# Adding each expert tile's rows to X in DRAM, instead of storing the tile and gathering two rows per token afterwards

## The chip, the cores and the metric

The kernel runs on one core of one Trainium2 chip. The metric is the device time of one execution in microseconds. The kernel before took 1797.72 us (median of 3 runs, 1793.24 to 1802.61).

## The reference, cut to what matters

Two layers over 1024 tokens of 1024 float32 features. Each layer has a mixer and then a mixture of 16 experts, of which every token takes 2; its two weighted results are added to x.

```python
def grouped_moe(h, router_w, router_bias, w_gate, w_up, w_down):
    ...
    _, idx = lax.top_k(masked, TOP_K)                    # 2 experts of one group
    ...
    a = jax.nn.silu(einsum(t, w_gate)) * einsum(t, w_up)
    y = jnp.einsum('tef,efd->td', a * gates[:, :, None], w_down)

for l in range(DEPTH):
    ...                                                  # mixer: x = x + g1 * y
    h = modulate(rms_norm(x, norm_ffn_g[l]), sh2, sc2)
    x = x + g2[:, None, :] * grouped_moe(h, ...)
return rms_norm(x, final_norm_g)
```

## The kernel before, in words

X stays in SBUF as 8 blocks of 128 tokens by 1024 features. The kernel is five programs, one for each engine (PE, VectorE = DVE, ScalarE = ACT, GpSimd = POOL, SyncE = SP), written by hand in program order; semaphores order them against each other. No scheduler moves anything.

**The expert stage of a layer.** DVE sorts the 2048 pairs of token and expert into tiles of 128 slots, one expert a tile (route, L1268). Here that gives 25 tiles in layer 0 and 26 in layer 1. A slot that no pair fills has token 0 and weight 0. The normed rows lie in DRAM (xn_scratch). For each tile POOL gathers its 128 rows of 4 KB into XG by an indirect DMA (L581). PE then runs this loop (L1050): gate and up products of tile t (L1015), transposes of tile t+1 (L996), down product of tile t-1 (L1030), transposes of tile t's hidden values (L1022). DVE multiplies the down product by the slot's weight and the layer's gate row into YS (L1435, L1437), one buffer of 512 KB. ACT stores YS into y_scratch, a DRAM tensor with a row per slot (L691). Before DVE writes YS again it waits for that store (L1433, y_out). SP loads the experts' weights, 3 MB each, into three buffers; it issues a load when the last tile of the expert in that buffer has its down product (L450).

**The stretch after the tiles.** POOL waits for the last store and issues 16 indirect gathers (L607): for each block of X the rows of its tokens' first and second slot. DVE adds both to the block (L1174 by combine). ACT sums each block's squares (L651) and takes roots four blocks at a time (L653). After layer 0, DVE scales four blocks (L1240), PE transposes them (L869), ACT and DVE evict the transposed half into HTR (L660, L1251), then the same for the second half; then the product with conf_w1 begins (L886). Its 16 items come in the order of w1_group: the first two need the first half of the tokens only. After layer 1, DVE writes scaled output blocks (L1244), four at a time, and SP stores them (L514).

**Other places that the change touches.** x_pieces on ACT (L698) reads the pieces of X that the mixer's output product finishes. At the start POOL writes zeros into the rows of y_scratch that a short run of tiles would leave unwritten (L561, 7.68 MB).

Of the kernel before, what the change touches and what calls it, by code (L numbers as in the profile page):

```python
# [7 lines left out]
F32 = mybir.dt.float32  # L8
I32 = mybir.dt.int32
U32 = mybir.dt.uint32  # L10
# [5 lines left out]
P = 128  # L16
# [4 lines left out]
NL = 2  # L21
# [108 lines left out]
def trunk(nc, i, out):  # L130
    with ExitStack() as ctx:
# [35 lines left out]
        TCUR = sb("TCUR", [P, 1], U32)  # L167
        RT = sb("RT", [1, 2 * MAXT], I32)
# [73 lines left out]
        def hv(n):  # L242
            return HTR[:, n, :]

        Y1, Y2 = ([HTR[:, 3 * n + b, :] for b in range(3)] + [R[:, 3 - n, b * D:(b + 1) * D] for b in range(4)]
                  for n in range(2))
        NY0, NY = 3, 7

        def y_of(b):

            return b if b < NY else NY0
# [11 lines left out]
        xn_dram = nc.dram_tensor("xn_scratch", (T, D), F32, kind="Internal").ap()  # L263
        y_dram = nc.dram_tensor("y_scratch", (MOST * P, D), F32, kind="Internal").ap()
# [38 lines left out]
        xup = sem("x_updated")  # L303
# [40 lines left out]
        c_in = [[[sem(f"combine_in{l}_{b}_{s}") for s in range(2)] for b in range(NB)] for l in range(NL)]  # L344
# [66 lines left out]
        def _(sp):  # L411
# [54 lines left out]
            sp.wait_ge(zeroed, 16 * (NH + 1))  # L466
            nt = experts(0)
            sp.wait_ge(dn[0], nt)
# [23 lines left out]
            for n in range(2):  # L492
                weights1(n)
# [6 lines left out]
            sp.wait_ge(c_in[0][NB - 1][1], 16)  # L500
# [10 lines left out]
            experts(1)  # L511
# [7 lines left out]
        def _(pool):  # L519
# [35 lines left out]
            rest = y_dram[LEAST * P:MOST * P, :].rearrange("(t p) d -> p t d", p=P)  # L555
            zeros = ZERO.unsqueeze(1).broadcast_to([P, MOST - LEAST, HT])

            for q in range(16):
                if q == 4:
                    for h in range(NH):  # L560
                        pool.dma_start(rest[:, :, HT * h:HT * h + HT], zeros).then_inc(zeroed, 16)  # L561
                    pool.dma_start(glu_dram.rearrange("(c p) t -> p c t", p=P)[:, :, 0:PADC],
                                   ZERO[:, 0:KC * PADC].rearrange("p (c t) -> p c t", c=KC)).then_inc(zeroed, 16)
# [6 lines left out]
            for l in range(NL):  # L570
# [7 lines left out]
                nt = pool.value_load(RT[0:1, 0:1], min_val=1, max_val=MOST)  # L578
# [5 lines left out]
                pool.tensor_tensor(PSCR[:, l:l + 1], PSCR[:, 2:3], PSCR[:, 2:3], ALU.add).then_inc(held[l], 1)  # L584
                pool.tensor_copy(TCUR[:], TOKI[:, 0:1]).then_inc(cur_ok[l], 1)
                pool.wait_ge(cur_ok[l], 1)
                gather()
                with pool.Fori(0, nt) as t:
# [4 lines left out]
                    pool.wait_ge(held[l], t + 1)  # L593

                    pool.tensor_tensor(PSCR[:, l:l + 1], PSCR[:, 2:3], PSCR[:, 2:3], ALU.add).then_inc(held[l], 1)
                    gather()

                pool.wait_ge(zeroed, 16 * (NH + 1))
                pool.wait_ge(y_out[l], nt * 16 + 16)
                pool.wait_ge(xg_in[l], nt * 16 + 16)  # L600
                pool.wait_ge(held[l], nt + 1)
                pool.tensor_tensor(PSCR[:, l:l + 1], PSCR[:, 2:3], PSCR[:, 2:3], ALU.add).then_inc(held[l], 1)
                for b in range(NB):
                    if b == NY:
                        pool.wait_ge(xup, 8 * l + NY0 + 1)
                    for s, dst in ((0, Y1), (1, Y2)):
                        pool.indirect_dma_start(  # L607
                            out=dst[y_of(b)], out_offset=None, in_=y_dram,
                            in_offset=bass.IndirectOffsetOnAxis(ap=SLOTU[:, s, b:b + 1], axis=0)
                        ).then_inc(c_in[l][b][s], 16)  # L610
# [14 lines left out]
        def _(act):  # L625
# [18 lines left out]
            def rms_sums(r, h):  # L644
# [3 lines left out]
                for b in range(4 * h, 4 * h + 4):  # L648
                    if r:
                        act.wait_ge(xup, 8 * (r // 2 - 1) + b + 1)  # L650
# [17 lines left out]
            def experts(l):  # L668
# [13 lines left out]
                act.sem_inc(y_out[l], 16)  # L682
# [6 lines left out]
                def store(t):  # L689
                    act.wait_ge(ys_d[l], t + 2)  # L690
                    act.dma_start(y_dram[bass.ds(t * P, P), :], YS).then_inc(y_out[l], 16)  # L691
                hidden(0)
                with act.Fori(1, nt) as t:
                    hidden(t)
                    store(t - 1)
                store(nt - 1)

            def x_pieces(l, g0):  # L698

                for p in range(4):  # L700
# [6 lines left out]
                    act.wait_ge(xpj, 16 * l + 4 * p + 4)  # L707
                    for b in (2 * p, 2 * p + 1):
# [47 lines left out]
            for h in range(NH):  # L756
                rms_sums(2, h)
            for h in range(NH):
                evict_ht(2, 1, 0, h)
            for n in range(16):  # L760
# [4 lines left out]
                act.activation(SIG[n % 2], take(g)[:], ACT.Sigmoid,  # L765
                               bias=PT[:, COL_B1 + KC + ct:COL_B1 + KC + ct + 1]).then_inc(free["A"], 1)
            act.wait_ge(conv_ok, KC)
# [24 lines left out]
            rms_sums(4, 0)  # L792
            rms_sums(4, 1)
# [3 lines left out]
        def _(pe):  # L797
# [307 lines left out]
            transposes(2, 1)  # L1105
# [31 lines left out]
            for n in range(16):  # L1137
                c, h = w1_group(n)
                ht_ready(2, h)
# [24 lines left out]
        def _(dve):  # L1164
# [68 lines left out]
            def rms_apply(r, h):  # L1233
# [4 lines left out]
                for b in range(4 * h, 4 * h + 4):  # L1238
                    if r < 4:
                        dve.tensor_scalar(XN[h][:, b % 4, :], X[:, b, :], RSTD[:, b:b + 1], None,  # L1240
                                          ALU.mult).then_inc(xn_ok, 1)
                        continue
# [431 lines left out]
```

## Time and profile before

| | us |
|---|---|
| median of 3 runs | 1797.72 |
| the profiled execution, its own time | 1794.08 |
| span in the profile, first to last instruction | 1792.3 |
| PE busy | 1525.7 (85%) |
| DVE busy | 855.2 (48%) |
| ACT busy | 257.8 (14%) |
| POOL busy | 146.8 (8%) |
| moved by DMA | 300.79 MB, mean 168 GB/s |

An engine's busy time is the sum of its instructions' durations, weight loads of PE apart. The granted clock is TensorE's, as a share of full speed. The start of a row is counted from the first instruction.

### The profile page before, as it was taken

Reading aid. Unit: us, or ns where it says so; the run is one execution under the profiler, and the core shown is the slowest. Engines: PE = TensorE matmul, PEld = TensorE weight load, DVE = VectorE, ACT = ScalarE, POOL = GpSimd, SP = SyncE. Lnnn points to the kernel's source line nnn. Section 1 sums busy time; section 2 is a strip of 40 time slices with the busy share of each in tenths; the row PEclk is TensorE's granted clock in tenths of the full one; section 3 lists DMA queues with packets and bytes.
Section 4 is the critical chain, followed back from the end, with each engine's and each line's share of the span. In section 5 each row is a group of like instructions: output and inputs, shape, how many; then the busy total and the mean of one; then the engine's idle time right before and its main releaser. Section 6 shows DMA issues by size and latency. Waiting matters only on the chain.

```text
span 1792.3 us, 16755 instructions
## 1 busy us (share of the span) xinstructions
PE 1525.7 (85%) x5355; PEld 851.1 (47%) x5356; DVE 855.2 (48%) x1546; ACT 257.8 (14%) x507; POOL 146.8 (8%) x267
## 2 busy tenths in 40 slices
PE   3899999989965999999459989987999389999980
PEld 2684544448853444444134434432887244444440
DVE  3554686644234223222352999975333523332226
ACT  2210000001121111111130000003212111111112
POOL 2000000000000111011210000000000101111104
PEclk9999999999986999999769989998999599999995
DMA  9575067460044666875532336433002658466827
GB/s 337 163 273 164 24 202 232 156 220 1 16 177 160 216 237 229 283 270 192 192 138 65 100 75 149 106 90 101 1 1 98 254 195 302 164 226 237 286 97 284
DMA packets 196430, 300.79 MB, mean 168 GB/s; under 512 B 12021, under 2 KB 153425, under 8 KB 196384
## 3 DMA queue, kind: packets, MB, share of 16 engines
q1 hardware_dynamic: 169952, 205.94, 36.6%
q0 software_dynamic: 17696, 62.24, 9.7%
q10 hardware_dynamic: 8736, 31.99, 4.5%
q8 instruction: 30, 0.49, 0.1%
q14 instruction: 16, 0.13, 0.0%
HBM read 248.51 MB, written 51.53 MB: 167 GB/s over the span
## 4 chain that ended last, share of the span: by engine, by line
PE 73%; DVE 13%; DMA 7%; ACT 2%; issue 2%; POOL 1%; SPq 0%; DVEq 0%; POOLq 0%; ACTq 0%
PE bank L886 19%; PE bank L1015 18%; PE bank L964 15%; PE bank L1030 9%; DVE W L1196 3%; DVE R L1620 3%; DMA W<-in_moe_w_down 3%; PE bank L996 3%; DVE R L1174 2%; PE bank L1122 1%; DMA W<-in_ada_w 1%; PE bank L869 1%; PE bank L1041 1%; PE bank L1155 1%; PE bank L903 1%
## 5 line engine op out<-in xcount | busy, mean ns | idle before, releaser
L886 PE MATMUL bank<-HTR,W 128*128 128x512 f32 x1024 | 449.8, 597 | 7.4 <-DVE R L1607 7.4
L1015 PE MATMUL bank<-W,R 128*128 x784 | 349.9, 600 | 17.8 <-DMA W<-in_moe_w_down 13.8
L886 PEld LDWEIGHTS bank<-HTR,W 128*128 128x128 f32 x1024 | 193.4, 191 | 243.8 <-issue 243.1
L1174 DVE TENSOR_TENSOR R<-bank,R 128x256 f32<-128x256 f32 (+1 forms) x91 | 49.3, 541 | 523.9 <-ACT R L686 322.3
L964 PE MATMUL bank<-W,R 128*128 128x256 f32 x1024 | 231.1, 385 | 9.0 <-ACT R L786 7.8
L1015 PEld LDWEIGHTS bank<-W,R 128*128 128x128 f32 x784 | 147.0, 193 | 186.2 <-issue 186.2
L964 PEld LDWEIGHTS bank<-W,R 128*128 128x128 f32 x1024 | 194.7, 193 | 38.6 <-ACT R L786 8.7
L1620 DVE SCALAR_TENSOR_TENSOR R<-R,PT 128x998 f32<-128x998 f32 (+21 forms) x152 | 195.0, 1283 | 5.4
L1030 PE MATMUL bank<-W,R 128*128 x408 | 185.4, 598 | 3.9 <-DVE R L1428 3.9
L1196 DVE SCALAR_TENSOR_TENSOR W<-W,CAB 128x256 f32<-128x256 f32 x308 | 149.3, 485 | 11.0
L1030 PEld LDWEIGHTS bank<-W,R 128*128 128x128 f32 x408 | 74.1, 192 | 78.4 <-issue 78.4
L1435 DVE SCALAR_TENSOR_TENSOR R<-bank,GSLOT,HTR 128x512 f32<-128x512 f32 x51 | 38.3, 751 | 121.8 <-PE bank L1030 121.8
L678 ACT ACTIVATE R<-bank,MC 128x128 f32<-128x128 f32 x212 | 79.7, 456 | 95.9 <-PE bank L996 95.9
L686 ACT ACTIVATE R<-bank 128x256 f32<-128x256 f32 x51 | 19.6, 384 | 477.6 <-PE bank L1015 459.9
L1411 DVE TENSOR_SCALAR R<-bank,MC 128x128 f32<-128x128 f32 x212 | 72.4, 403 | 18.6 <-PE bank L996 18.6
L869 PE MATMUL bank<-IDENT,R 128*128 128x128 f32 x128 | 28.0, 386 | 62.2 <-DVE R L1240 45.7
L1174 DVE TENSOR_TENSOR R<-R 128x512 f32<-128x512 f32 (+8 forms) x146 | 64.5, 461 | 24.6 <-ACT R L751 21.3
L996 PEld LDWEIGHTS bank<-IDENT,R 128*128 128x128 f32 x424 | 51.0, 144 | 42.9 <-issue 26.9
L996 PE MATMUL bank<-IDENT,R 128*128 128x128 f32 x424 | 56.8, 278 | 15.6 <-DMA R<-xn_scratch,TCUR 15.6
L964 PE MATMUL bank<-W,HTR 128*128 128x256 f32 x256 | 59.9, 394 | 2.4 <-ACT HTR L660 1.4
L869 PEld LDWEIGHTS bank<-IDENT,R 128*128 128x128 f32 x128 | 21.1, 197 | 71.1 <-issue 35.0
L964 PEld LDWEIGHTS bank<-W,HTR 128*128 128x128 f32 x256 | 50.0, 198 | 10.1 <-issue 1.9
(194 smaller groups left out, 972.5 us busy)
## 6 DMA issues: line engine op xcount, KB each, us to landing
W<-in_ada_w SPq DMA_DIRECT2D x48, 1024.0 KB, 11.5
W<-in_moe_w_gate SPq DMA_DIRECT2D x32, 1024.0 KB, 7.6
W<-in_moe_w_up SPq DMA_DIRECT2D x32, 1024.0 KB, 11.3
W<-in_moe_w_down SPq DMA_DIRECT2D x32, 1024.0 KB, 13.5
y_scratch<-R ACTq DMA_DIRECT2D x51, 512.0 KB, 7.4
W<-glu_scratch SPq DMA_DIRECT2D x48, 258.0 KB, 4.7
W<-in_conf_w SPq DMA_DIRECT2D x12, 1024.0 KB, 8.8
W<-in_hyb_w_in SPq DMA_DIRECT2D x10, 1024.0 KB, 13.1
```

The lines of the kernel that those rows point to most:

```text
L678: ins = act.activation(XT[:, k, :], TB_[0][:, k * P:(k + 1) * P], ACT.Identity, bias=MC[:, l, 3, k:k + 1], scale=MC[:, l, 2, k:k + 1])
L869: ins = pe.transpose(TB_[q % 2][:, P * b:P * b + P], XN[h][:, b, P * k:P * k + P], IDENT[:])
L886: ins = pe.matmul(dst[:], lhs(k), rhs(k), start=(k == 0), stop=(k == kc - 1))
L964: ins = pe.matmul(dst[:, QW * b:QW * b + QW], src[:, k, t0:t0 + P], w[:, k, :], start=(k == 0), stop=(k == KC - 1))
L996: ins = pe.transpose(TB_[k // 4][:, P * (k % 4):P * (k % 4) + P], XG[:, P * k:P * k + P], IDENT[:])
L1015: ins = pe.matmul(M[0][:], XT[:, k, :], W[:, bass.ds(at + k * 2 * FE, 2 * FE)], start=(k == 0), stop=(k == KC - 1))
L1030: ins = pe.matmul(M[1 + h][:], AT[:, k, :], W[:, bass.ds(at + 2 * KC * FE + k * D + h * HT, HT)], start=(k == 0), stop=(k == 1))
L1174: return dve.tensor_tensor(o, a, b, op)
L1196: ins = dve.scalar_tensor_tensor(out=acc, in0=w[:, k, :], scalar=CAB[:, k, 0:1], in1=acc, op0=ALU.mult, op1=ALU.add)
L1411: ins = dve.tensor_scalar(XT[:, k, :], TB_[1][:, (k - 4) * P:(k - 3) * P], MC[:, l, 2, k:k + 1], MC[:, l, 3, k:k + 1], ALU.mult, ALU.add)
L1435: dve.scalar_tensor_tensor(out=YS[:, 0:HT], in0=M[1][:], scalar=g, in1=GBF[:, 0:HT], op0=ALU.mult, op1=ALU.mult)
L1620: link(dve.scalar_tensor_tensor(out=o[:, d:T], in0=p[:, 0:T - d], scalar=tap(CTAPS - 1 - d), in1=o[:, d:T], op0=ALU.mult, op1=ALU.add))
```

## The change

DRAM now holds a copy of X (xsum_scratch), which ACT writes from SBUF while the mixer finishes X. After each expert tile POOL adds the 128 rows of YS to the rows of that copy by one indirect DMA that accumulates. It does so after it has issued the gather of the tile three further on. YS is still one buffer, and DVE waits before it for the previous add. Two adds never overlap, since POOL waits for the one before. Empty slots now point at 128 spare rows behind the 1024 real ones, a row of its own for each partition, in both scratch tensors, so that no row occurs twice in a tile. The loop runs over the tiles but two (more = tiles - 2), and two adds follow it. After the last add SP loads X's 8 blocks back. y_scratch, its zeros, the ACT stores, the 16 gathers and the 16 additions of DVE are gone. In layer 0 the second half's transposes and evictions move behind the first two items of the conf_w1 product. At the end roots, scaling and output go block by block.

```diff
@@ POOL, expert tiles
-                with pool.Fori(0, nt) as t:
+                def next_tile(t):
                     pool.wait_ge(xg_in[l], t * 16 + 16)
                     pool.tensor_copy(TCUR[:], TOKI[:, bass.ds(t + 1, 1)]).then_inc(cur_ok[l], 1)
                     pool.wait_ge(cur_ok[l], t + 2)
                     pool.wait_ge(xtr[l], t + 1)
...
-                pool.wait_ge(y_out[l], nt * 16 + 16)
-                for b in range(NB):
-                    for s, dst in ((0, Y1), (1, Y2)):
-                        pool.indirect_dma_start(
-                            out=dst[y_of(b)], out_offset=None, in_=y_dram,
...
+                def add_rows(t):
+                    pool.wait_ge(y_out[l], t * 16 + 16)
+                    pool.tensor_copy(TSUM[:], TOKI[:, bass.ds(t, 1)]).then_inc(sum_cur[l], 1)
+                    pool.wait_ge(sum_cur[l], t + 1)
+                    pool.wait_ge(ys_d[l], t + 2)
+                    met()
+                    pool.indirect_dma_start(
+                        out=xs_dram, out_offset=bass.IndirectOffsetOnAxis(ap=TSUM[:, 0:1], axis=0),
+                        in_=YS, in_offset=None, compute_op=ALU.add).then_inc(y_out[l], 16)
...
+                next_tile(0)
+                next_tile(1)
+                pool.wait_ge(x_out[l], 16 * 4)
+                with pool.Fori(0, more) as t:
+                    next_tile(t + 2)
+                    add_rows(t)
+                add_rows(more)
+                add_rows(more + 1)
@@ ACT, per tile
-                def store(t):
-                    act.wait_ge(ys_d[l], t + 2)
-                    act.dma_start(y_dram[bass.ds(t * P, P), :], YS).then_inc(y_out[l], 16)
@@ ACT, x_pieces
+                    act.dma_start(xs_dram[2 * P * p:2 * P * (p + 1), :].rearrange("(b q) d -> q b d", q=P),
+                                  X[:, 2 * p:2 * p + 2, :]).then_inc(x_out[l], 16)
@@ SP
+            def reload(l, nt, b):
+                if b == 0:
+                    sp.wait_ge(y_out[l], nt * 16 + 16)
+                sp.dma_start(X[:, b, :], xs_dram[P * b:P * b + P, :]).then_inc(x_back[b], 16)
             nt = experts(0)
-            sp.wait_ge(dn[0], nt)
-            for n in range(2):
-                weights1(n)
+            for b in range(NB):
+                reload(0, nt, b)
+                if b == 3:
+                    for n in range(2):
+                        weights1(n)
@@ PE, after layer 0
             transposes(2, 0)
-            transposes(2, 1)
             for n in range(16):
+                if n == 2:
+                    transposes(2, 1)
@@ DVE, route: spare rows for empty slots
+                tokr = SM[:, 0:16].rearrange("p (s b) -> p s b", s=TOPK)
+                link(dve.tensor_scalar(SPARE[:], TOKF[:, 0:1], float(T), None, ALU.add))
+                for s in range(TOPK):
+                    dve.scalar_tensor_tensor(out=tokr[:, s, :], in0=TOKF[:], scalar=-float(T),
+                                             in1=rf.rearrange("p (s b) -> p s b", s=TOPK)[:, s, :],
+                                             op0=ALU.add, op1=ALU.subtract).then_inc(dch, 1)
@@ DVE, the end
+            def last_norm(b):
+                dve.wait_ge(fin_sd, b + 1)
+                link(dve.reciprocal(RSTD[:, b:b + 1], SD[:, b:b + 1]))
+                dve.scalar_tensor_tensor(out=OUTS[b], in0=X[:, b, :], scalar=RSTD[:, b:b + 1],
+                                         in1=FGB, op0=ALU.mult, op1=ALU.mult).then_inc(out_ok, 1)
```

The order of POOL's instructions in layer 0, from the loop over the tiles to the end of the stage. Before, TCUR and PSCR are the small copies around a gather, and y_scratch is read in two runs behind the loop:

```order
L590 COPY TCUR<-TOKI 128x1
L591 REGISTER_ALU
L595 TENSOR_TENSOR PSCR<-PSCR 1x1
L581 DMA R<-xn_scratch,TCUR 128x1024
L588 REGISTER_ALU
L588 COMPARE_AND_BRANCH
L599 ISA
L601 REGISTER_ALU
L602 TENSOR_TENSOR PSCR<-PSCR 1x1
L607 DMA HTR<-y_scratch,SLOTU 128x1024 x6
L607 DMA R<-y_scratch,SLOTU 128x1024 x10
```

After the change, in the same place, the loop and the first of the two adds behind it:

```order
L598 COPY TCUR<-TOKI 128x1
L599 REGISTER_ALU
L593 TENSOR_TENSOR PSCR<-PSCR 1x1
L588 DMA R<-xn_scratch,TCUR 128x1024
L606 ISA
L607 ISA
L607 COPY TSUM<-TOKI 128x1
L608 REGISTER_ALU
L593 TENSOR_TENSOR PSCR<-PSCR 1x1
L611 DMA xsum_scratch<-R,TSUM 1152x1024
L622 REGISTER_ALU
L622 COMPARE_AND_BRANCH
```

Each turn of the loop now issues a gather and, behind it on the same queue, an add; the 16 gathers behind the loop have become two adds.

The order of PE's instructions between the experts of layer 0 and the conf_w1 product, before (the transposes are the rows with IDENT, the product those with HTR, and L1122 is the first convolution by PE):

```order
L1030 MATMUL bank<-W,R 128x512
L1056 REGISTER_ALU
L869 MATMUL bank<-IDENT,R 128x128 x64
L886 MATMUL bank<-HTR,W 128x512 x64
L1122 MATMUL bank<-W 32x512 x16
```

And after the change:

```order
L1050 MATMUL bank<-W,R 128x512
L1076 REGISTER_ALU
L889 MATMUL bank<-IDENT,R 128x128 x32
L906 MATMUL bank<-HTR,W 128x512 x32
L889 MATMUL bank<-IDENT,R 128x128 x32
L906 MATMUL bank<-HTR,W 128x512 x32
L1142 MATMUL bank<-W 32x512 x16
```

Half of the 64 transposes now stand behind the first 32 matmuls of the product.

## Rows read from the trace of the kernel before

**Rows 1.** The page, busy time of PE: us, share of the span, instructions.
```profile
PE 1525.7 (85%) x5355; PEld 851.1 (47%) x5356; DVE 855.2 (48%) x1546; ACT 257.8 (14%) x507; POOL 146.8 (8%) x267
```
**Rows 2.** Chain of waits: start us, us, what; the last store of either layer.
```profile
873.45 7.08 DMA y_scratch<-R
...
1745.73 2.67 DMA y_scratch<-R
```
**Rows 3.** Timeline after layer 0's tiles: start us, us, engine, line, operation [idle before].
```profile
866.66 0.74 DVE L1437 SCALAR_TENSOR_TENSOR R<-bank,GSLOT,HTR 128x512 f32<-128x512 f32 x1
...
871.87 0.75 DVE L1435 SCALAR_TENSOR_TENSOR R<-bank,GSLOT,HTR 128x512 f32<-128x512 f32 x1 [4.14 <-PE bank L1030]
...
881.37 0.96 POOL L607 DMA_INDIRECT HTR<-y_scratch,SLOTU  x1 [0.51 <-issue]
...
898.27 1.06 ACT L651 ACTIVATE R<-X 128x1024 bf16<-128x1024 f32 x1 [1.52 <-DVE X L1174]
...
899.44 1.28 ACT L653 ACT_TABLE_LOAD   x1
...
901.35 4.03 DVE L1240 TENSOR_SCALAR R<-X,RSTD 128x1024 f32<-128x1024 f32 x4
...
924.60 6.76 PE L869 MATMUL bank<-IDENT,R 128*128 128x128 f32 x28 [3.77 <-DVE R L1240]
...
932.09 13.47 PE L886 MATMUL bank<-HTR,W 128*128 128x512 f32 x31
```
**Rows 4.** Windows: stretch, its length, busy us of each engine, granted clock, DMA share, GB/s.
```profile
740.00:800.00 60.00, 51.91 (x144) 24.64 (x144) 15.72 (x35) 7.54 (x20) 5.55 (x13) 0.94 0.84 287
...
872.00:905.00 33.00, 0.00 (x0) 0.00 (x0) 17.21 (x17) 7.33 (x12) 19.05 (x19) 0.57 0.94 312
```
**Rows 5.** Timeline of the end, after layer 1's tiles.
```profile
1737.24 0.74 DVE L1437 SCALAR_TENSOR_TENSOR R<-bank,GSLOT,HTR 128x512 f32<-128x512 f32 x1
...
1744.15 0.75 DVE L1435 SCALAR_TENSOR_TENSOR R<-bank,GSLOT,HTR 128x512 f32<-128x512 f32 x1 [5.83 <-PE bank L1030]
...
1771.53 17.79 SPq L514 DMA_DIRECT2D out<-R  x8
...
1784.09 4.87 DVE L1244 SCALAR_TENSOR_TENSOR R<-X,RSTD,HTR 128x1024 f32<-128x1024 f32 x4
```
**Rows 6.** DMA by line: issues, size, median us from issue to landing.
```profile
W<-in_moe_w_down SPq DMA_DIRECT2D x32, 1024.0 KB, 13.5
y_scratch<-R ACTq DMA_DIRECT2D x51, 512.0 KB, 7.4
...
HTR<-gate_scratch ACTq DMA_DIRECT2D x2, 512.0 KB, 3.8
```
**Rows 7.** The gathers of tiles (tile TCUR): time to landing of all 53.
```profile
DMA to landing us min/median/max: 4.0/4.6/7.8
```
**Rows 8.** Timeline of one expert tile in layer 0.
```profile
831.80 0.75 DVE L1435 SCALAR_TENSOR_TENSOR R<-bank,GSLOT,HTR 128x512 f32<-128x512 f32 x1 [2.28 <-PE bank L1030]
...
836.83 0.18 POOL L590 COPY TCUR<-TOKI 128x1 uint32 x1 [6.96 <-DMA R<-xn_scratch,TCUR]
...
838.47 1.04 PE L996 MATMUL bank<-IDENT,R 128*128 128x128 f32 x8
...
839.16 0.42 DVE L1174 TENSOR_TENSOR R<-bank,R 128x256 f32<-128x256 f32 x1 [5.62 <-ACT R L686]
...
843.20 0.75 DVE L1435 SCALAR_TENSOR_TENSOR R<-bank,GSLOT,HTR 128x512 f32<-128x512 f32 x1 [2.28 <-PE bank L1030]
```
**Rows 9.** Waits: PE in the gate and up products, us in total, times, longest.
```profile
PE bank L1015 <- DMA W<-in_moe_w_down: 13.8, 4, 4.4
```
**Rows 10.** Chain of waits: the first gate and up product of layer 0.
```profile
566.77 9.97 PE bank L1041 x16
```
**Rows 11.** Timeline of DVE at the start of layer 0's route.
```profile
524.37 0.18 DVE L1499 RECIPROCAL RSTD<-SD 128x4 f32<-128x4 f32 x1 [1.43 <-ACT SD L712]
```

More of the change, by code:

```diff
@@ L243, in hv @@
             return HTR[:, n, :]
[L245 to L251, printed above, removed]
         GBF = hv(6)
@@ L343, in trunk @@
         y_out = [sem(f"tile_stored{l}") for l in range(NL)]
-        c_in = [[[sem(f"combine_in{l}_{b}_{s}") for s in range(2)] for b in range(NB)] for l in range(NL)]
+        x_out = [sem(f"x_rows_stored{l}") for l in range(NL)]
+        x_back = [sem(f"x_block_reloaded{b}") for b in range(NB)]
+        sum_cur = [sem(f"sum_tokens_copied{l}") for l in range(NL)]
+        fin_sd = sem("final_root_ready")
         out_ok = sem("output_block_ready")
@@ L466, in _ @@
             sp.wait_ge(zeroed, 16 * (NH + 1))
+            for l in range(NL):
+                sp.wait_ge(y_out[l], 16)
+            def reload(l, nt, b):
+                if b == 0:
+                    sp.wait_ge(y_out[l], nt * 16 + 16)
+                sp.dma_start(X[:, b, :], xs_dram[P * b:P * b + P, :]).then_inc(x_back[b], 16)
             nt = experts(0)
-            sp.wait_ge(dn[0], nt)
             def weights1(n):
@@ L510, in _ @@
             sp.wait_ge(free["D"], emptied(GROUPS["var"] - 1))
-            experts(1)
+            nt = experts(1)
+            for b in range(NB):
+                reload(1, nt, b)
             for b in range(NB):
@@ L560, in _ @@
                     for h in range(NH):
-                        pool.dma_start(rest[:, :, HT * h:HT * h + HT], zeros).then_inc(zeroed, 16)
+                        s = slice(HT * h, HT * h + HT)
+                        pool.dma_start(xn_dram[T:T + P, s], ZERO).then_inc(zeroed, 16)
+                        pool.dma_start(xs_dram[T:T + P, s], ZERO).then_inc(y_out[h], 16)
                     pool.dma_start(glu_dram.rearrange("(c p) t -> p c t", p=P)[:, :, 0:PADC],
@@ L577, in _ @@
                 pool.wait_ge(xn_out[l], 16 * NB)
-                nt = pool.value_load(RT[0:1, 0:1], min_val=1, max_val=MOST)
+                more = pool.value_load(RT[0:1, 1 + NE:2 + NE], min_val=0, max_val=MOST - 2)
                 def gather():
@@ L583, in gather, with met @@
                         in_offset=bass.IndirectOffsetOnAxis(ap=TCUR[:, 0:1], axis=0)).then_inc(xg_in[l], 16)
[L584 to L587, printed above, removed]
-                with pool.Fori(0, nt) as t:
+                def met():
+                    pool.tensor_tensor(PSCR[:, l:l + 1], PSCR[:, 2:3], PSCR[:, 2:3], ALU.add).then_inc(held[l], 1)
+                def next_tile(t):
                     pool.wait_ge(xg_in[l], t * 16 + 16)
@@ L754, in _, with gate1 @@
             experts(0)
[L756 to L760, printed above, removed]
+            def gate1(n):
                 g = GROUPS["w1"] + 2 * n
@@ L766, in _ @@
                                bias=PT[:, COL_B1 + KC + ct:COL_B1 + KC + ct + 1]).then_inc(free["A"], 1)
+            rms_sums(2, 0)
+            evict_ht(2, 1, 0, 0)
+            rms_sums(2, 1)
+            for n in range(16):
+                if n == 2:
+                    evict_ht(2, 1, 0, 1)
+                gate1(n)
             act.wait_ge(conv_ok, KC)
@@ L791, in _ @@
             experts(1)
-            rms_sums(4, 0)
-            rms_sums(4, 1)
+            for b in range(NB):
+                act.wait_ge(x_back[b], 32)
+                link(act.activation(JUNK, X[:, b, :], ACT.Square, accum_out=SS[:, b:b + 1]))
+                act.activation(SD[:, b:b + 1], SS[:, b:b + 1], ACT.Sqrt, bias=EPSC[:],
+                               scale=1.0 / D).then_inc(fin_sd, 1)
         @block.tensor
@@ L1402, in route @@
                 link(dve.tensor_copy(GSLOT[:], X0[:, MAXT:2 * MAXT]))
-                dve.tensor_copy(TOKI[:], X0[:, 0:MAXT]).then_inc(tab_ok, 1)
+                dve.tensor_scalar(TOKI[:], X0[:, 0:MAXT], SPARE[:], None, ALU.add).then_inc(tab_ok, 1)
             def experts(l):
@@ L1594, in _ @@
             experts(0)
-            for b in range(NB):
-                if b == 5:
-                    rms_apply(2, 0)
-                combine(0, b)
+            rms_apply(2, 0)
             evict_ht(2, 1, 0, 0)
             rms_apply(2, 1)
-            evict_ht(2, 1, 0, 1)
             for n in range(16):
```

62 lines of the change are left out of this document (22 added, 40 removed).

## The prediction

> **What bounds the kernel now.** I read the page's busy times first: PE is busy for 85% of the span [rows 1]. So the change can only pay where PE stands still. The chain of waits then says where. It runs through PE except in a few places, and two of these are the last stores into y_scratch and what follows them [rows 2]. In the first place PE does nothing at all from 872 to 905, while DMA is at its limit: 312 GB/s and a busy share of 0.94, with a mean granted clock of 0.57 [rows 4]. The timeline shows that the conf_w1 product starts only at 932.09 [rows 3]. The end of the kernel has the same shape and nothing after it: 46.7 us from the last YS (1745.6) to the end of the span at 1792.3 [rows 5]. In the tiles a period is 11.4 us, bounded by PE: DVE writes YS at 831.80 and again at 843.20 [rows 8]. DMA is slower than PE there in four places only, where PE waits 13.8 us in all for the weights [rows 9].
>
> **The unknown: one add.** No row shows an accumulating DMA. Let L be its time from POOL's start of it to landing. On an idle chip a gather of the same 512 KB takes 4.0 us at least [rows 7], and a store of 512 KB 2.67 us [rows 2]. An add has to read the old rows and write the new ones. So one row gives the lower bound, 4.0, and for the idle case I take the usual gather and the store one behind the other: about 4.4 + 2.7 = 7.1 us. The upper bound is the slowest gather and the usual store beside weight loads, 7.8 + 7.4 = 15.2 us [rows 6, 7].
>
> The Trainium skill, "DMA: Bandwidth & Descriptors", section "Anatomy of one DMA", fits about 2.0 us plus bytes over 436 GB/s for a DMA issued by GpSimd and puts most of the 2 us on the write receipt. An estimate by it, with the rows read and written once each, is 2.0 + 2.4 us plus about 1 us on POOL, 5.4 us in all. No run here shows it, and by it both terms for the gaps below would be larger by about 3.4 us each.
>
> **The gap after layer 0.** The last YS but one ends at 866.66 + 0.74 = 867.40 [rows 3]. POOL then needs 0.1 to wake, 0.18 for its small instruction and 0.51 from there to the start of the DMA [rows 3, 8], so the add starts at 868.2 and lands at 875.3. DVE has one YS, so its last L1435 starts at 875.4 where it started at 871.87, 3.5 later. YS is done after 1.4 us, the last add starts at 877.5 and lands at 884.6. SP issues the reload at 884.8. The first block lands after 3.8 us, as the loads of 512 KB from DRAM do [rows 6], and the next every 1.7 us (0.524 MB at 312 GB/s [rows 4]): the fourth at 893.7. The four sums follow the blocks, and the last takes 1.25 us; then come the table load of 1.28, the root of 0.3, a reciprocal of 0.2, and four scalings in 4.0 [rows 3]: 900.7. Transposes and evictions of a half took 924.60 to 932.09, 7.5 us. The product begins at 908.2 instead of 932.09: 23.9 us earlier. Its two weight slices are queued behind block 3 and land by 893.7 + 6.7 = 900.4, in time.
>
> Two things are given back. The second half, 7.5 us, now stands in the middle of the product. It is no later than that: its blocks land by 907.1 and its scaling ends near 918, while PE comes to it at 908.2 + 27.6. And the product now starts sooner after PE's idle time, in which the granted clock has a mean of 0.57, near the lower of its levels (1.2 of 2.4 GHz) [rows 4]. The first gate and up product of layer 0, after a similar wait, took 9.97 us [rows 10] where 16 such matmuls at the full clock take 6.95 (13.47 for 31 [rows 3]), so 3.0. Sum: 23.9 - 7.5 - 3.0 = **13.4 us gained**.
>
> **The end.** The same steps from 1737.98 [rows 5]: the add lands at 1745.9, L1435 starts at 1746.0 instead of 1744.15, the last add lands at 1755.3, and the reload is issued at 1755.4. By the engines alone the eighth block would land at 1771.0, take 1.25 + 0.3 + 0.2 + 1.2 us in ACT and DVE, and its store 3.3 (the last one of before, 1789.0 to 1792.3): 1777.3. But 4.19 MB come in and 4.19 MB go out on one SP queue, and 8.39 MB at 312 GB/s are 26.9 us. With 2.1 us before the first bytes and 1 at the end that is 1785.4. I take DMA as the bound: **6.9 us gained**; the engines' bound would be 15.
>
> **The tiles.** POOL has room: it waits nearly the whole period. The add of tile t is issued 0.8 us after YS, behind the gather in POOL's order, so it delays no gather's issue. ACT loses its store, which nothing waited for. The wait in front of YS is the one that can bite. The loop add, YS, add needs L + 1.4 + 0.8 in a period of 11.4, so L may be 9.2 on average. Single adds may be later: DVE idles for 5.6 us after each tile [rows 8], which is its slack. Beside weight loads a store takes 7.4 us against 2.67, so I put a loaded add at 11 and an idle one at 7.1. About half the tiles are loaded (13 loads in 25 and 26 tiles), which gives a mean of 9.1, just inside. I cost the loop at 0.
>
> What it does cost is bandwidth. In the four weight waits the loads have 287 GB/s and a DMA share of 0.84 [rows 4, 9], and one tile's output is in each such load. Reading the old rows adds 0.524 MB, 1.8 us, four times: **7.3 us lost**. Elsewhere a load has 22.8 us or more for 13.5 [rows 6]; that spare time hides it.
>
> **The small edits.** Three more DVE instructions on 8 or 16 columns precede the one-hots in the chain that PE and POOL wait for, 0.2 us each, as the reciprocal on 8 columns takes [rows 11], in two layers: 1.2. The last copy of X's pieces puts an ACT DMA issue of about 0.35 in front of the sums for which DVE waits (1.43 us of idle time [rows 11]): 0.7. Both together **1.9 lost**. The 7.68 MB of zeros go, but PE waits for no DMA at that time: 0. The copies of X, 4.19 MB in each layer, lie beside products that leave DMA mostly idle: 0.
>
> **Sum.** -13.4 - 6.9 + 7.3 + 1.9 = -11.1 us from the profiled execution's own 1794.08: 1783. That execution is 3.6 us under the median, so from the median it would be 1786.6. I forecast 1785. Each us of L counts four times, since each gap holds two adds: at L = 4.0 the DVE waits vanish and the sum is 1773, and without the bandwidth term 1766; at an idle L of 9.2 it is 1791.
>
> **The rivals.**
> *The add becomes the loop's bound (slower).* Place: DVE's wait for y_out before L1435, then PE's down product. It decides from a mean L of 9.2. At a mean of 10 it costs 0.8 x 51 tiles = 41 us and 12 more in the gaps: 1836. With both upper bounds (15.2 loaded, 9.2 idle: mean 12.2) it is 3.0 x 51 = 153 and more, over 1900. For it: my mean of 9.1 stands a tenth under the limit, and a loaded store takes nearly three times an idle one. Against it: the fastest stores leave a wide margin.
> *The gather becomes late (slower).* A gather now queues behind an add on POOL's queue. At 836.83 it had landed and at 838.47 PE used it: 1.6 us of slack in a loaded tile [rows 8]. If the add delays it by 3 us, 26 loaded tiles lose 1.4 each, 36 us: 1819.
> *The gaps gain little (no change).* If reloads and stores behind the adds run at less than the gathers' rate, or the clock stays low for longer in the conf_w1 product, some 10 us of the gain go: 1794.
> *A short add (faster still).* L near 5 and an end where both directions overlap: 1783 - 8 - 5 = 1770.
>
> For the second the Trainium skill speaks too: "DMA: Bandwidth & Descriptors", section "Queues, rings and completion order", says that within a queue of one DMA engine descriptors are taken in order, while different queues take turns packet by packet. The stores of before had ACT's queue for themselves, and the adds share POOL's with the gathers. Whether that costs anything no row of before shows, as nothing else was on that queue during the tiles.
>
> **How the numbers follow.** The forecast has 0.40, with its own range of 1776 to 1793; the late add 0.22, the late gather 0.10, little gained 0.17, the short add 0.11. A measurement of this kernel can't tell less than 0.5%, 9 us, from no change: faster means under 1788.7, slower over 1806.7. Of the forecast 0.32 lies under 1788.7 and 0.08 above. Faster: 0.32 + 0.11 + a little of the others = 0.45. Slower: the two slow rivals, and some of what I can't see of an operation that no row shows, 0.35. The same: 0.20. The range goes from the short add to a mean L a little over 10, 1768 to 1845.
>
> **What would show it.** Right: adds that land in about 7 us where no weights load and 11 where they do; no wait of DVE before YS that PE feels; L1435 of the last tiles later by 3.5 and 1.8 us; the conf_w1 product starting some 31 us after the last YS instead of 59; the end taking 38 us from the last YS. Wrong: a tile period over 11.4 us with DVE waiting for the add, PE's transposes waiting for gathers, or weight waits far over 13.8 + 7.3 us. The forecast is wrong above all if L is not what a gather and a store make together.

## The result, and the profile after

The changed kernel takes 1768.44 us (median of 4 runs, 1763.36 to 1769.91) beside 1795.48 for the kernel before on the same chip (4 runs, 1792.55 to 1802.61): ratio 0.985, 95% interval 0.983 to 0.988. Five more runs later, beside other variants, gave 1767.63 and a ratio of 0.983 (0.981 to 0.985). The profiled execution took 1768.09 us with a span of 1766.3, so 26.0 us less in either than before. The sum of the prediction was 11.1 less from that base. The sign was right, the size was less than half of what came.

The page's busy times of the changed kernel, against [rows 1]: PE does the same work, and DVE and POOL exchange some.

```profile
PE 1524.5 (86%) x5355; PEld 848.0 (48%) x5356; DVE 818.0 (46%) x1528; ACT 259.1 (15%) x513; POOL 214.0 (12%) x388
```

The timeline after layer 0's tiles, for [rows 3]: start, duration, engine and line, and in brackets the idle time before and what ended it.

```profile
879.23 0.75 DVE L1460 SCALAR_TENSOR_TENSOR R<-bank,GSLOT,HTR 128x512 f32<-128x512 f32 x1 [6.42 <-DMA xsum_scratch<-R,TSUM]
879.90 0.74 DVE L1462 SCALAR_TENSOR_TENSOR R<-bank,GSLOT,HTR 128x512 f32<-128x512 f32 x1
...
881.06 1.57 POOL L611 DMA_INDIRECT xsum_scratch<-R,TSUM  x1 [0.16 <-issue]
887.26 1.77 SPq L470 DMA_DIRECT2D X<-xsum_scratch  x4
...
890.61 1.06 ACT L668 ACTIVATE R<-X 128x1024 bf16<-128x1024 f32 x1 [21.68 <-DMA X<-xsum_scratch]
...
898.65 2.74 DVE L1261 TENSOR_SCALAR R<-X,RSTD 128x1024 f32<-128x1024 f32 x4
901.64 4.63 PE L889 MATMUL bank<-IDENT,R 128*128 128x128 f32 x20 [24.94 <-DVE R L1261]
...
909.75 27.70 PE L906 MATMUL bank<-HTR,W 128*128 128x512 f32 x64 [0.95 <-issue]
937.29 1.04 PE L889 MATMUL bank<-IDENT,R 128*128 128x128 f32 x8
```

YS of the last tile is done at 880.64 and the conf_w1 product begins 29.1 us later, where it was 58.8 [rows 3]. The second half's transposes stand behind its first 64 matmul records (the trace has two records for each of these 32 instructions). The end, for [rows 5]:

```profile
1734.21 0.75 DVE L1460 SCALAR_TENSOR_TENSOR R<-bank,GSLOT,HTR 128x512 f32<-128x512 f32 x1 [6.14 <-DMA xsum_scratch<-R,TSUM]
...
1736.04 1.58 POOL L611 DMA_INDIRECT xsum_scratch<-R,TSUM  x1 [0.16 <-issue]
1741.86 3.87 SPq L470 DMA_DIRECT2D X<-xsum_scratch  x8
...
1749.56 10.09 SPq L522 DMA_DIRECT2D out<-R  x8
...
1758.00 1.28 DVE L1476 SCALAR_TENSOR_TENSOR R<-X,RSTD,HTR 128x1024 f32<-128x1024 f32 x1
```

From the last YS (1735.62) to the end of the span (1766.3) it is 30.7 us, where it was 46.7. Windows of the same kernel (columns as in [rows 4]): a loaded stretch of tiles, three pieces of the gap, and the end.

```profile
740.00:800.00 60.00, 49.21 (x135) 23.46 (x135) 13.56 (x31) 7.01 (x19) 12.79 (x25) 0.89 0.89 280
893.00:901.00 8.00, 0.00 (x0) 0.00 (x0) 2.53 (x5) 4.16 (x8) 0.00 (x0) 0.50 1.06 365
901.00:905.00 4.00, 3.34 (x14) 2.73 (x15) 1.20 (x2) 1.02 (x2) 0.00 (x0) 0.50 1.03 409
905.00:909.00 4.00, 3.14 (x20) 1.98 (x18) 1.78 (x3) 2.48 (x4) 0.00 (x0) 0.91 0.52 78
1749.00:1758.00 9.00, 0.00 (x0) 0.00 (x0) 8.75 (x15) 8.30 (x19) 0.00 (x0) 0.50 1.00 376
```

Then the adds themselves (tile TSUM: POOL's own time in ns, min, median and max; who waited for them; time to landing), and PE's wait for the weights, for [rows 9]:

```profile
L611 POOL DMA_INDIRECT xsum_scratch<-R,TSUM x51: 1572/1614/1640, 596.1 to 1736.0; - x51
...
  DVE R L1460: 95.7, 24
...
DMA to landing us min/median/max: 5.8/9.7/11.1
```
```profile
PE bank L1035 <- DMA W<-in_moe_w_down: 20.3, 4, 5.6
```

The gathers of the tiles (tile TCUR), for [rows 7]:

```profile
DMA to landing us min/median/max: 3.8/4.4/7.8
```

Two neighbouring tiles on POOL show how the landings divide. The adds begin at 618.84 and 632.14. The first lands beside a weight load and wakes POOL at 629.92, 11.1 us later; the second, without one, at 638.82, 6.7 us later.

```profile
618.84 1.61 POOL L611 DMA_INDIRECT xsum_scratch<-R,TSUM  x1 [0.50 <-issue]
...
629.92 0.18 POOL L607 COPY TSUM<-TOKI 128x1 uint32 x1 [3.79 <-DMA xsum_scratch<-R,TSUM]
632.14 1.61 POOL L611 DMA_INDIRECT xsum_scratch<-R,TSUM  x1 [0.50 <-issue]
...
638.82 0.18 POOL L607 COPY TSUM<-TOKI 128x1 uint32 x1 [1.29 <-DMA xsum_scratch<-R,TSUM]
```

**Where the 26.0 us come from**, by stages of the two profiled executions (us, after less before):

| stage | change |
|---|---|
| up to the first gather (557.94, now 560.22) | +2.3 |
| layer 0, first gather to last YS (315.3, now 320.4) | +5.1 |
| last YS to conf_w1 product (58.8, now 29.1) | -29.7 |
| conf_w1 product, with half the transposes in it | +7.0 |
| the rest of the second mixer | -2.2 |
| layer 1's tiles (325.2, now 332.7) | +7.5 |
| last YS to the end (46.7, now 30.7) | -16.0 |

The sum is -26.0. The two rows of tiles are best read together. The kernel before has 640.5 us in both, and a profile with the same tile code (the new order alone, below) has 640.1, but split as 310.9 and 329.3. The changed kernel has 653.1, and 652.1 in its second profile. The 2.2 us of the second mixer vary from profile to profile: they lie between the end of the conf_w1 product and the mixer's last product, 61.2 us here and 63.4 before, and the second profile of the changed kernel has 63.2.

### The profile page after: what moved, and what is told of

Its sections match the earlier page's. It is cut to its first block and busy times, and to the rows that moved or that the text cites. A ratio compares the mean times of both kernels' runs of the same rounds, so it can differ in the third digit from the quotient of the medians.

```text
span 1766.3 us, 16888 instructions
## 1 busy us (share of the span) xinstructions
PE 1524.5 (86%) x5355; PEld 848.0 (48%) x5356; DVE 818.0 (46%) x1528; ACT 259.1 (15%) x513; POOL 214.0 (12%) x388
## 5 line engine op out<-in xcount | busy, mean ns | idle before, releaser
L1035 PE MATMUL bank<-W,R 128*128 x784 | 354.4, 606 | 24.3 <-DMA W<-in_moe_w_down 20.3
L984 PE MATMUL bank<-W,R 128*128 128x256 f32 x1024 | 230.9, 384 | 9.0 <-ACT R L803 7.8
L984 PEld LDWEIGHTS bank<-W,R 128*128 128x128 f32 x1024 | 194.5, 192 | 38.5 <-ACT R L803 8.7
L1460 DVE SCALAR_TENSOR_TENSOR R<-bank,GSLOT,HTR 128x512 f32<-128x512 f32 x51 | 38.3, 751 | 157.4 <-DMA xsum_scratch<-R,TSUM 95.7
L611 POOL DMA_INDIRECT xsum_scratch<-R,TSUM x51 | 82.2, 1611 | 24.9 <-issue 24.9
L1016 PEld LDWEIGHTS bank<-IDENT,R 128*128 128x128 f32 x424 | 51.0, 144 | 42.2 <-issue 26.9
L1016 PE MATMUL bank<-IDENT,R 128*128 128x128 f32 x424 | 56.8, 278 | 15.0 <-DMA R<-xn_scratch,TCUR 15.0
L593 POOL TENSOR_TENSOR PSCR<-PSCR 1x1 f32<-1x1 f32 x104 | 19.0, 183 | 361.3 <-PE bank L1016 195.8
L889 PE MATMUL bank<-IDENT,R 128*128 128x128 f32 x128 | 23.9, 338 | 43.6 <-DVE R L1261 32.8
L984 PE MATMUL bank<-W,HTR 128*128 128x256 f32 x256 | 59.2, 391 | 2.4 <-ACT HTR L677 1.4
## 6 DMA issues: line engine op xcount, KB each, us to landing
W<-in_moe_w_down SPq DMA_DIRECT2D x32, 1024.0 KB, 14.6
```

Source lines behind the costliest of these rows:

```text
L611: pool.indirect_dma_start(out=xs_dram, out_offset=bass.IndirectOffsetOnAxis(ap=TSUM[:, 0:1], axis=0), in_=YS, in_offset=None, compute_op=A ...
L984: ins = pe.matmul(dst[:, QW * b:QW * b + QW], src[:, k, t0:t0 + P], w[:, k, :], start=(k == 0), stop=(k == KC - 1))
L1016: ins = pe.transpose(TB_[k // 4][:, P * (k % 4):P * (k % 4) + P], XG[:, P * k:P * k + P], IDENT[:])
L1035: ins = pe.matmul(M[0][:], XT[:, k, :], W[:, bass.ds(at + k * 2 * FE, 2 * FE)], start=(k == 0), stop=(k == KC - 1))
L1460: dve.scalar_tensor_tensor(out=YS[:, 0:HT], in0=M[1][:], scalar=g, in1=GBF[:, 0:HT], op0=ALU.mult, op1=ALU.mult)
```

## The experiments

Each kernel is the changed one with one edit, unless said otherwise. A ratio is always to the kernel before on the same chip. Each edit is shown cut to what matters; "..." marks left-out lines.

**The new order undone.** The second half's transposes and evictions stand ahead of the conf_w1 product again.

```diff
@@ PE; the evictions of ACT and DVE move in the same way
             transposes(2, 0)
+            transposes(2, 1)
...
             for n in range(16):
...
-                if n == 2:
-                    transposes(2, 1)
```

> The changed kernel, but with the second half's transposes and evictions of layer 0 in front of the conf_w1 product again, as before the change; the adds and reloads stay. Computes the reference. Theory (the gaps pay, step by step): the second half is scaled at 916.5 in the changed kernel's trace, so the product starts at about 924 instead of 909.8, and saves the 7.0 us in its middle: the stage ends 7 us later, 1775. Rival 1 (the order alone brings the gain of the gap): 1785 or more, over 16 us later. Rival 2 (the order brings nothing, as its 7 us are only moved): within 1 us of the changed kernel.

Measured: 1776.14 us (1772.72 to 1778.72), ratio 0.990 (0.987 to 0.992), against 0.983 to 0.988 for the change; about 8 us of the gain go, as the first theory said, and neither rival fits. The last YS ends at 881.63, and the product begins 43.6 us after it (29.1 in the changed kernel), with no transposes in it:

```profile
925.19 30.21 PE L905 MATMUL bank<-HTR,W 128*128 128x512 f32 x70
```

**The new order alone.** The kernel before, with only that edit of PE, ACT and DVE.

```diff
@@ the kernel before, PE
             transposes(2, 0)
-            transposes(2, 1)
...
             for n in range(16):
...
+                if n == 2:
+                    transposes(2, 1)
```

> The kernel before, with only the new order at the conf_w1 product (second half's transposes and evictions behind its first two items). Computes the reference. Theory: the 16 gathers still pace the gap, the first half is evicted at about 921.6 and DVE still has three blocks to add in between, so the product starts some 10 us earlier than 932.1 and gives 7 back: 1 to 5 us gained, 1792. Rival (the order is what makes the gap short): 15 us or more gained, 1780.

Measured: 1790.58 us (1786.15 to 1796.27, 10 runs), ratio 0.999 (0.997 to 1.000). Its product begins earlier than before:

```profile
914.35 27.70 PE L887 MATMUL bank<-HTR,W 128*128 128x512 f32 x64 [0.95 <-issue]
```

From the last YS (868.36) to the product it is 46.0 us, 12.8 less than before, of which the transposes inside the product take 7 back. The time is 3.6 us less, with an interval that ends at no change, inside the 1 to 5 of the theory. So the two halves of the gap's gain can be told apart: the reload without the order brings 58.8 - 43.6 = 15.2 us, the order 14.5 - 7.0 = 7.5 on top of it.

**A plain scatter.** The same DMA without the addition, so the sums are missing.

```diff
-                        in_=YS, in_offset=None, compute_op=ALU.add).then_inc(y_out[l], 16)
+                        in_=YS, in_offset=None).then_inc(y_out[l], 16)
```

> The changed kernel with compute_op left out: each tile's rows overwrite the rows of the copy in DRAM and are not added, so the output is not the reference's. Same POOL instructions and waits, no reading of old rows. Theory: the old rows' reading is 0.52 MB more per tile; without it a transfer lands in 4 to 5 us instead of 5.8 to 6.3 on an idle chip and in 7 to 9 instead of 10.8 to 11.1 beside loads; PE's waits for weights fall from 20.3 us back to about 14, and the four idle adds around the gaps give 1.3 us each: 1757 in all. Rival (an accumulating transfer costs as much as a plain one, and its time is descriptor work on POOL): landing times and the 20.3 us stay, 1768.

Measured: 1728.67 us, ratio 0.963 (0.959 to 0.966). The total can't be used: with other values in X, layer 1 is routed into 24 tiles and not 26. Layer 0 is the same work, and there the trace shows the price of accumulating. The rows are the two kinds of the transfer and, of this kernel, PE's weight waits in layer 0 alone.

```profile
L611 POOL DMA_INDIRECT xsum_scratch<-R,TSUM x49: 985/1002/1011, 597.1 to 1699.2; - x49
...
DMA to landing us min/median/max: 3.3/7.5/9.7
```
```profile
PE bank L1035 <- DMA W<-in_moe_w_down: 5.1, 3, 3.3
```

A plain scatter costs POOL 1.00 us where an add costs 1.61, and lands 2.5 us sooner when idle (least values) and 1.4 beside weights (largest values). The rival, a plain transfer as dear as an add, is out. The weight waits of layer 0 are 5.1 us, with adds 10.8. From the first gather to the start of the last transfer layer 0 takes 310.6 us, with adds 320.8. Some 10 us of the changed kernel's layer 0 are thus the price of accumulating. This is one profile, and layer 0's tiles differ by 4.5 us between the two profiles with the tile code of before (315.3 and 310.9); the seven profiles with one add per tile in the loop's usual order agree within 1 us (319.6 to 320.5 to the last YS).

**Two adds per tile.** A second scratch tensor gets the same 512 KB added, and DVE and POOL wait for both.

```diff
+                    pool.indirect_dma_start(
+                        out=zs_dram, out_offset=bass.IndirectOffsetOnAxis(ap=TSUM[:, 0:1], axis=0),
+                        in_=YS, in_offset=None, compute_op=ALU.add).then_inc(z_out[l], 16)
...
@@ DVE, before YS
+                        dve.wait_ge(z_out[l], t * 16 + 16)
```

> The changed kernel with a second add of the same 512 KB per tile into a second scratch tensor that nobody reads; DVE and POOL wait for both. Computes the reference. Theory (the loop add, YS, add hides as long as the mean landing time is under 9.2 us): both together land in about 9 us idle and 15 loaded, a mean of 12, so every tile is 2 to 3 us longer, PE waits for DVE's tile output, and the time is 1768 + 51 x 2.8 + gaps 12 + weights 8 = 1930 (1880 to 1960). Rival (there is slack for more, the adds' time in the loop is free): only weights and gaps grow, under 1800.

Measured: 1856.89 us (1851.73 to 1859.11), ratio 1.034 (1.031 to 1.037). The loop's bound exists: DVE now waits in nearly every tile, and PE for the gathers behind two adds.

```profile
DVE R L1470 <- DMA second_sum_scratch<-R,TSUM: 377.2, 47, 11.7
...
PE bank L1025 <- DMA R<-xn_scratch,TCUR: 54.4, 25, 8.1
```
```profile
705.51 0.75 DVE L1470 SCALAR_TENSOR_TENSOR R<-bank,GSLOT,HTR 128x512 f32<-128x512 f32 x1 [9.69 <-DMA second_sum_scratch<-R,TSUM]
...
732.63 0.75 DVE L1470 SCALAR_TENSOR_TENSOR R<-bank,GSLOT,HTR 128x512 f32<-128x512 f32 x1 [8.91 <-DMA second_sum_scratch<-R,TSUM]
```

Two tiles take 27.1 us here, 22.8 with one add. Both of my expectations were off. It isn't free, and it costs a little over half of what I said. From the start of the first add to the landing of the second it is 11.1 us in the mean of 51 tiles, 1.9 over the limit of 9.2, where I had taken 12 and so 2.8: the loaded pairs land in 12 to 14.6 us and not in 15.

**The add ahead of the gather.**

```diff
                 with pool.Fori(0, more) as t:
-                    next_tile(t + 2)
                     add_rows(t)
+                    next_tile(t + 2)
```

> The changed kernel with one thing exchanged: in POOL's loop the add of tile t now stands ahead of the gather of tile t+3 and not behind it. Theory that the order of the two makes it cheap: the add waits for YS, so the gather is issued some 6 us later in each tile, and it shares the queue and the DMA engines with an add under way; a gather had 1.6 us of slack in a loaded tile, so PE waits for gathers by 2 to 8 us per tile, 100 to 300 us in all, 1870 to 2070. Rival: the rings take turns and the gather's own slack is larger than I read (it is issued two tiles ahead), so that it costs under 1 us per tile: below 1800.

Measured: 2087.63 us in one run, 289 over the kernel before. The gather is issued only when YS is done, 2.2 us behind the start of the add, and PE waits for it in almost every tile. The rows: PE's total wait, one tile, and the landings of the gathers.

```profile
PE bank L1016 <- DMA R<-xn_scratch,TCUR: 273.2, 49, 8.5
```
```profile
713.64 1.61 POOL L611 DMA_INDIRECT xsum_scratch<-R,TSUM  x1 [0.16 <-issue]
...
715.87 1.02 POOL L588 DMA_INDIRECT R<-xn_scratch,TCUR  x1 [0.15 <-issue]
...
721.11 1.09 PE L1016 MATMUL bank<-IDENT,R 128*128 128x128 f32 x8 [2.47 <-DMA R<-xn_scratch,TCUR]
```
```profile
DMA to landing us min/median/max: 4.1/6.3/11.1
```

The mean wait, 5.6 us, lies in the range I gave; the total lies above it. PE's busy time also grows, from 1524.5 to 1607.4 us, at a mean granted clock of 0.896 where the changed kernel has 0.94. The run shows the late issue and the landing behind an add together and doesn't part them.

**One store at the end.**

```diff
-            for b in range(NB):
+            for b in range(NB - 1, NB):
```

> The changed kernel with seven of the eight output stores left out (most of the output is not written), the last block's store kept. Theory that DMA bounds the end: in the changed kernel the last store was issued at 1759.6 and the span ended 6.7 us later, where an undisturbed store takes 3.3; without the 3.67 MB ahead of it the store lands in 3.3 us and the reload of the last blocks lands sooner too, so the end is 3.5 to 5 us earlier. Theory that the engines bound it (reload, sum, root, scaling of the last block): the end moves by under 1 us.

Measured: 1766.39 us (1765.00 to 1767.79), ratio 0.983 (0.981 to 0.985), not distinguishable from the changed kernel's beside it. The trace is finer. The last scaling begins 23.0 us after the last YS, as in the changed kernel run beside it (23.2), and the span ends 3.0 us after the issue of the store, at 1763.2, which is 27.3 us after the last YS. The changed kernel needs 30.0 there, and 30.7 in its first profile.

```profile
1742.40 4.01 SPq L470 DMA_DIRECT2D X<-xsum_scratch  x8
...
1758.86 1.28 DVE L1476 SCALAR_TENSOR_TENSOR R<-X,RSTD,HTR 128x1024 f32<-128x1024 f32 x1
1760.17 0.34 SPq L522 DMA_DIRECT2D out<-R  x1
```

The stores that queue up cost about 3 us, a little less than the 3.5 to 5 of the theory; without them the engines (reload, then 1.37 us per block on ACT) end at 20.8 us from the first reload, where the changed kernel takes 24.4.

**The end by fours.** Sums, roots and scaling of the end as before the change, behind the same reload.

```diff
@@ ACT; DVE's last_norm goes back to four blocks at a time too
-            for b in range(NB):
-                act.wait_ge(x_back[b], 32)
...
+            rms_sums(4, 0)
+            rms_sums(4, 1)
```

> The changed kernel with the end undone alone: roots, reciprocals, scaling and output go four blocks at a time again, as before the change, behind the same reload. My theory after the run with one store: DMA bounds the end from the first store on (8.39 MB in 24.4 us from the first reload), and the engines need 20.8 us for the same stretch. By fours the first store waits for four blocks' sums (some 4 us later than 1749.6), and DMA stands idle for part of that time; so the end takes 2 to 4 us more than the 30 to 30.7 us from the last YS: 1770 to 1772. Rival: the order at the end is worth nothing, since the total of bytes decides: no difference to 1768. Should it cost over 6 us, then a good part of what I put down to the shorter reload belongs to this edit.

Measured: 1767.37 us (1765.36 to 1771.68), ratio 0.984 (0.980 to 0.988): the rival was right. The first store is issued 19.2 us after the last YS (1732.31), not 13.9, and the end still comes 31.3 us after it, at 1763.6, at most 1.3 later than in the changed kernel's two profiles.

```profile
1738.99 4.08 SPq L470 DMA_DIRECT2D X<-xsum_scratch  x8
...
1751.52 8.91 SPq L522 DMA_DIRECT2D out<-R  x8
```

**Roots block by block in the gap too**, and ACT loads the root's table while it waits, in both places. This was meant to beat both kernels.

```diff
@@ ACT, the gap; DVE's reciprocals and scalings there go block by block too
-            rms_sums(2, 0)
...
+            root_table()
+            for b in range(4):
+                one_root(b, 1)
             evict_ht(2, 1, 0, 0)
-            rms_sums(2, 1)
+            for b in range(4, 8):
+                one_root(b, 1)
```

> The changed kernel with two additions, meant to be faster than both: after layer 0 roots, reciprocals and scalings go block by block as they already do at the end, and ACT loads the table for the root (1.28 us) while it still waits for the adds, in both places. My theory: in the gap after layer 0 the last scaling of the first half ended at 901.39 with block 3's sum ended at 896.8; now it should end about 1.6 us after the sum (0.3 root, 0.2 reciprocal, 0.7 scaling and the hand-overs), so the conf_w1 product starts about 3 us earlier, some 26 us after the last YS instead of 29.1. At the end the first store starts 1.3 us earlier, and as the DMA works without a pause from there, the end comes up to 1.3 us earlier. Sum 3 to 4.5 us: 1764 where the changed kernel has 1768. Rival: the first half is bound by DMA, or what is won comes back as a wait for the weights or the second half's blocks; then no difference to the changed kernel.

Measured: 1765.21 us (1763.67 to 1767.62), ratio 0.982 (0.980 to 0.984), beside 1767.63 and 0.983 for the changed kernel. The same kernel a second time:

> Roots block by block after layer 0 and the root's table loaded while ACT waits, a second time, since 1765.2 against 1767.6 could not be told apart by the first. The gap after layer 0 was 3.7 us shorter in its trace and the end no shorter, so I expect 3 to 4 us under the changed kernel, a ratio of about 0.982 where the changed kernel had 0.983 to 0.985. Rival: what the gap gains comes back later; then 0.9835 to 0.985.

Measured: 1766.33 us (1764.58 to 1770.87), ratio 0.984 (0.981 to 0.987). So its time can't be told from the changed kernel's, and the 3 to 4.5 us that I forecast do not show in it. In the trace the gap is shorter: the last scaling of the first half ends at once behind its root, and the product begins 25.3 us after the last YS (878.90), 25.9 in the second profile, instead of 29.1 and 28.8.

```profile
894.79 0.16 DVE L1632 RECIPROCAL RSTD<-SD 128x1 f32<-128x1 f32 x1 [0.41 <-ACT SD L781]
894.99 0.75 DVE L1633 TENSOR_SCALAR R<-X,RSTD 128x1024 f32<-128x1024 f32 x1
896.03 5.60 PE L900 MATMUL bank<-IDENT,R 128*128 128x128 f32 x24 [20.88 <-DVE R L1633]
...
904.15 27.70 PE L917 MATMUL bank<-HTR,W 128*128 128x512 f32 x64 [0.95 <-ACT HTR L678]
```

At the end the first store is issued 13.2 us after the last YS and the end comes at 31.5 and 30.3: nothing gained, as with the end by fours.

```profile
1737.76 4.05 SPq L471 DMA_DIRECT2D X<-xsum_scratch  x8
...
1744.51 11.33 SPq L523 DMA_DIRECT2D out<-R  x8
```

## Why the prediction was right in kind and short in size

**What held.** The time is near that of my last rival, a short add and both directions overlapping (1770), which I had given 0.11. That is in part luck: an idle add is 5.8 to 6.7 us and not near 5, and of the surplus 3.0 us come from the clock, of which that rival says nothing. The loop of add, YS, add fits in the period: loaded and idle adds often alternate, up to 11.1 us (I took 11) and 5.8 to 6.7 (I took 7.1), a mean of 8.2 under the limit of 9.2. DVE waits 95.7 us for them in 24 tiles, and PE does not feel it except through the last YS of each layer, 2.3 and 2.0 us late (I said 3.5 and 1.8): the last L1460 begins 2.5 and 2.25 us after its down product, before 0.25. The two adds per tile show that the limit is real. The late-gather rival is out: 37 of the changed kernel's 53 gathers are issued while an add is in flight, 4 to 7 us behind its start, and their landings are 3.8/4.4/7.8 us in all, as before [rows 7]. The exchanged order shows what the order gather, add avoids, a gather that has to wait until YS is done. From the start of the mixer's last product (L984, 1239.42) to layer 1's first gather it is 163.47 us, before 163.48, and 163.4 to 164.2 in nine profiles with the small DVE edits; what these cost there is under a microsecond.

**The bandwidth.** I took 7.3 us for the weight waits. The waits grew by 6.5 (20.3 less 13.8 [rows 9]), and the two tile stages by 12.6, less 4.3 for the late last YS: 8.3. The second profile of the changed kernel has 21.6 us of such waits, 6.4 of them put down to the gate weights. The term holds, and the plain scatter shows its cause in layer 0.

**First failed term: the gap, 13.4 predicted, 20.4 measured** (29.7 less 7.0 and 2.3). 3.0 of the 7.0 us is the charge for a cold clock in the conf_w1 product. It began at once at full clock, 27.70 us for 64 matmuls, where [rows 3] has 13.47 for 31. The low clock fell on the transposes ahead of it: granted 0.50 from 901 to 905, where 20 of them took 4.63 us, and 0.91 from 905 to 909. The transposes of before, from which I took the 7.5 us, had been at the low clock as well:

```profile
925.00:929.00 4.00, 3.98 (x18) 3.03 (x17) 1.10 (x2) 1.55 (x2) 0.00 (x0) 0.50 0.00 0
```

So I had paid for the clock in the 7.5 us already and charged it twice. What it really costs there is small: a half with its evictions takes 8.1 us from 901.64 to 909.75, and 7.0 at full clock in the middle of the product. The rest is many small pieces. The add needs 6.2 us from its start to SP's issue (1.1 less than the 7.1 + 0.2 I took), the blocks come half a us sooner, and four scalings without the old additions between them take 2.74 us where they took 4.03 (1.3 less). The late YS is 1.2 less and the second half 0.5; the first half's transposes are 0.6 more.

**Second failed term: the end, 6.9 predicted, 14.0 measured** (16.0 less 2.0 for the late YS). I had the right bound and the wrong rate for it. From the first reload's issue I allowed 30.0 us for 8.39 MB, at the 312 GB/s of [rows 4]; it took 24.4, which is 344 GB/s with the latencies in it. The 312 were a mean over a stretch with a pause in it, between the last store and the first gather's data, and with many small packets ahead of the pause. The same trace of before has 363 in the stretch's last 12 us:

```profile
893.00:905.00 12.00, 0.00 (x0) 0.00 (x0) 10.62 (x11) 5.86 (x10) 9.68 (x10) 0.50 0.98 363
```

By that row the term would have been 23.1 + 3.1 = 26.2 us and the end 3.8 us earlier. Even that rate is low. The changed kernel's second profile moves 412 GB/s for 18 us of its end, reloads and stores together, and the first has 376 for nine:

```profile
1748.00:1766.00 18.00, 0.00 (x0) 0.00 (x0) 10.95 (x16) 12.06 (x25) 0.00 (x0) 0.50 1.02 412
```

The Trainium skill, "DMA: Bandwidth & Descriptors", section "Where 436 GB/s comes from", has about 358 GB/s as the limit of one core's transfers from and to HBM; by it the bytes alone would take 23.4 us. The 363 of that row are near it, but the 412 here are above it, and the measurement decides. The last add, 5.8 us instead of 7.1, and shorter hand-overs give another 1.8. That DMA is the bound is shown by three kernels: the first store 5 us later (by fours) or 0.7 us sooner (table ahead) moves the end by 1.5 us at most, while seven stores fewer take 3 us off. From first reload to end the eight profiles with adds and all stores have 23.6 to 25.1 us, the one with a single store 20.8.

The Trainium skill, "DMA: Bandwidth & Descriptors", section "Anatomy of one DMA", gave an estimate of 5.4 us for an idle add with each row read and written once. The trace has 5.8 as the least, so the page was nearer than my gather plus store. Accumulating adds 2.5 us here to a plain scatter's 3.3.

**What is open.** The first stage was 2.3 us longer, and I had 1.9 for the edits in it. But eight variants with the same code in that stage have their first gather at 558.45 to 561.78, and the kernel before with only the new order at 557.5: the added steps cost between 1 and 4 us, and my 1.9 can be neither confirmed nor refuted closer than that. The 2.2 us that the rest of the second mixer gained differ from profile to profile of the same kernel, and why is open. How far an add may be late before PE feels it was not measured with a second YS buffer: that version wasn't tried.

## What to carry to other kernels

A gap in which the bounding engine stands still is worth more than its own row: read all that lies in it (last landing, reload, sums, roots, first product) as one chain, and charge a slow clock once, at the first work behind each pause, after a look at whether the row that the price comes from already has it. A DMA rate is read from a stretch with the same kind of transfers in the same directions, since a bound by bytes moves the whole term. When a queue gets a second, later-waiting user, place the transfer that the bounding engine needs next ahead of the wait.

## What the runs showed of the hardware

An accumulating indirect DMA of 128 rows by 4 KB takes 1.6 us of POOL and lands in 5.8 us at least; the plain one takes 1.0 and 3.3. Beside weight loads the two come nearer: 11.1 and 9.7 us at most. Two adds in flight together to different tensors take 11.1 us on average from the start of the first to the landing of the second, one alone 8.2. Reads and writes at once move hardly more bytes than reads alone: 376 GB/s from 1749 to 1758 and 412 over 18 us of the second profile, where reloads and stores overlap, against 365 and 409 in the gap from 893 to 901 and from 901 to 905, where no store runs. The granted clock rose from 0.50 to 1.00 while PE did nothing but transposes with pauses between them; in all variants the product behind them ran at full clock from its first matmul.
